# Split activations 192 instead of 64 bytes past the weight slots' phase, token-major weight tiles 192 bytes into their slots, one weight tile for both mLSTM gates

## What is computed

```python
def mlstm_mixer(h, w_in, w_if, b_if, head_norm, w_o):
    q, k, v, o_pre = jnp.split(h @ w_in, [hq, 2 * hq, 2 * hq + hv], axis=-1)
    gates = (h @ w_if + b_if).astype(jnp.float32)       # 1024 -> 2 * 4 heads
    gates = GATE_CAP * jnp.tanh(gates / GATE_CAP)
    log_i = _to_chunks(gates[..., :ML_HEADS], ML_HEADS, 1)[..., 0]
    log_f = _to_chunks(jax.nn.log_sigmoid(gates[..., ML_HEADS:]), ML_HEADS, 1)[..., 0]
    ...
def sqrelu_mlp(h, w1, w2):
    return jnp.square(jax.nn.relu(h @ w1)) @ w2
```

## Time and profile before

| | |
|---|---|
| median of 3 runs | 1549.48 us (1549.19 to 1552.05) |
| the profiled execution | 1549.48 us, its span 1547.7 us |
| PE busy | 1537.4 us (99%), 12836 matmuls |
| DVE, ACT, POOL busy | 1044.9 us (68%), 849.9 us (55%), 122.8 us (8%) |
| DMA | 281.05 MB, 182 GB/s on average |
| granted TensorE clock | 1.00 in every stretch of the windows shown |

### The profile page before, as it was taken

One profiled execution on the slowest core, in us unless ns is written; L12 is line 12 of the kernel. 1 busy time (PEld: TensorE's weight loads), 2 busy tenths in 40 slices (PEclk: granted clock), 3 DMA queues, 4 the chain that ended last, 5 costly groups with the idle time before them and its releaser, 6 DMA issues.

```text
span 1547.7 us, 35180 instructions
## 1 busy us (share of the span) xinstructions
PE 1537.4 (99%) x12836; PEld 1497.8 (97%) x12836; DVE 1044.9 (68%) x1765; ACT 849.9 (55%) x1301; POOL 122.8 (8%) x123
## 2 busy tenths in 40 slices
PE   9999999999999999999999999999999999999999
PEld 8899999988999999999999999999999988999999
DVE  7777765643876557666788766668566666687764
ACT  6776654546655445445445544556555547665543
POOL 1830000036000000000000000000000023200000
DMA  7146556554555566666665665656556981066664
GB/s 253 62 134 195 194 188 202 172 169 147 182 197 195 188 197 190 196 193 199 195 208 190 197 194 192 205 181 204 193 193 195 224 219 66 15 203 191 194 200 150
DMA packets 80784, 281.05 MB, mean 182 GB/s; under 512 B 8880, under 2 KB 12464, under 8 KB 80688
## 3 DMA queue, kind: packets, MB, share of 16 engines
q1 hardware_dynamic: 76800, 274.82, 55.3%
q10 hardware_dynamic: 3888, 4.85, 1.7%
HBM read 278.06 MB, written 1.57 MB: 181 GB/s over the span
## 4 chain that ended last, share of the span: by engine, by line
PE 95%; DVE 3%; ACT 1%; issue 1%; POOL 0%; ACTq 0%; DVEq 0%; POOLq 0%
PE psum L1760 27%; PE psum L1764 27%; PE psum L1761 27%; PE psum L1902 2%; PE psum L1904 2%; PE psum L1903 2%; PE psum L2194 1%; PE psum L2145 1%; PE psum L2259 1%; PE psum L2178 1%; PE psum L2090 0%; PE psum L1967 0%; PE psum L1957 0%; DVE w_lo L1039 0%; PE psum L1974 0%
## 5 line engine op out<-in xcount | busy, mean ns | idle before, releaser
L566 ACT ACTIVATE w_hi<-raw 128x1024 fp32r<-128x1024 f32 x518 | 547.2, 1058 | 478.8 <-PE psum L1764 421.7
L1039 DVE TENSOR_TENSOR w_lo<-raw,w_hi 128x1024 fp32r<-128x1024 f32 x483 | 590.5, 1223 | 246.2 <-ACT w_hi L566 245.8
L1760 PE MATMUL psum<-xs,w_hi 128*128 128x256 f32 x1912 | 530.7, 278 | 0.0
L1761 PE MATMUL psum<-xs,w_hi 128*128 128x256 f32 x1912 | 528.3, 276 | 0.0
L1764 PE MATMUL psum<-xs,w_lo 128*128 128x256 f32 x1912 | 528.2, 276 | 0.0
L1760 PEld LDWEIGHTS psum<-xs,w_hi 128*128 128x128 f32 x1912 | 358.9, 188 | 0.5 <-DVE w_lo L1039 0.2
L1761 PEld LDWEIGHTS psum<-xs,w_hi 128*128 128x128 f32 x1912 | 358.9, 188 | 0.3
L1764 PEld LDWEIGHTS psum<-xs,w_lo 128*128 128x128 f32 x1912 | 358.8, 188 | 0.0
L1764 PE MATMUL psum<-hs,w_lo 128*128 128x256 f32 x1280 | 353.3, 276 | 0.0
L1760 PE MATMUL psum<-hs,w_hi 128*128 128x256 f32 x1280 | 353.3, 276 | 0.0
L1761 PE MATMUL psum<-hs,w_hi 128*128 128x256 f32 x1280 | 353.3, 276 | 0.0
(11 more groups left out here) (292 smaller groups left out, 1487.4 us busy)
## 6 DMA issues: line engine op xcount, KB each, us to landing
raw<-tiles SPq DMA_DIRECT2D x518, 512.0 KB, 4.2
bias<-bias_dram ACTq DMA_DIRECT2D x8, 256.0 KB, 8.3
x<-x_in SPq DMA_DIRECT2D x4, 256.0 KB, 5.1
w1c_all<-w1c_k ACTq DMA_DIRECT2D x4, 256.0 KB, 4.4
w1c_all<-w1c_v ACTq DMA_DIRECT2D x4, 256.0 KB, 5.1
y_out<-x SPq DMA_DIRECT2D x8, 128.0 KB, 3.4
con<-consts SPq DMA_DIRECT2D x1, 803.0 KB, 8.8
bias_dram<-bias_row ACTq DMA_DIRECT2D x1, 512.0 KB, 7.1
```

Of the source, the lines that this page charges most:

```text
L566: act.activation(w_hi[s][:, :], raw[s][:, :], ACT.Copy).then_inc(hi_ready, 1)
L1039: dve.tensor_tensor(w_lo[s][:, :], raw[s][:, :], hi_of(w_hi[s][:, :]), ALU.subtract).then_inc(lo_ready, 1)
L1760: pe.matmul(out, w_hi[s][:, c:c + P], x_hi, start=first, stop=False)
L1761: pe.matmul(out, w_hi[s][:, c:c + P], x_lo, start=False, stop=False)
```

## The change

- Two spare regions of the layout change: `w_hi` and `w_lo` slots grow from 4096 to 4352 bytes (`SLOT`), `sil` is now the first two buffers of `half` (2048 bytes less), and `apart` shrinks by 128 bytes. The slots still begin at 128 modulo 256; `os_`, `xs`, `hs` and `arena` now begin at 64, which is 192 past the slots.
- Tiles of token-major stages lie 192 bytes into their slots (`TILE_AT`, `ASIDE`), so at phase 64, that of the activations. The first four tiles of kv and of nq stay at the slot's start. Of the 486 token-major matmuls 96 work on those.
- The offset from the activations to the moving operand changes so: in the feature form, moving minus stationary was 64 and is 192. In the token-major form it was 192 and is 0 (64 for the 96).
- Both gates come from one tile (`gates`: input gates in columns 0 to 3, forget gates in columns 32 to 35), so from one PSUM bank, at partitions 0 and 32. 517 tiles are left. mgate and mqk are one `feature` call of nine outputs, in which the gates' tile is paired with the first mqk tile.

```diff
+F_GATES = 32
-    ("mgate", 2, 2), ("mqk", 8, 8), ("mv", 8, 4), ("mo", 8, 4), ("wo_m", 8, 8),
+    ("mgate", 1, 1), ("mqk", 8, 8), ("mv", 8, 4), ("mo", 8, 4), ("wo_m", 8, 8),
...
+SLOT = TILE + 64
+ASIDE = 48
+TILE_AT = {}
 for _name, _tiles, _outs in STAGES:
     TILE0[_name], OUT0[_name] = N_TILES, N_OUTS
+    if _name in ("uk", "uq", "uv", "mv", "mo", "kv", "nq"):
+        for _t in range(RING if _name in ("kv", "nq") else 0, _tiles):
+            TILE_AT[N_TILES + _t] = ASIDE
+def slot_part(buffer, t):
+    first = TILE_AT.get(t, 0)
+    return buffer[:, first:first + TILE]
...
-        w_hi = [sb(f"w_hi{s}", [P, TILE], F32R) for s in range(RING)]
-        w_lo = [sb(f"w_lo{s}", [P, TILE], F32R) for s in range(RING)]
+        w_hi = [sb(f"w_hi{s}", [P, SLOT], F32R) for s in range(RING)]
+        w_lo = [sb(f"w_lo{s}", [P, SLOT], F32R) for s in range(RING)]
-        sil = [sb(f"sil{s}", [P, S]) for s in range(2)]
+        sil = half[0:2]
-        sb("apart", [P, 120])
+        sb("apart", [P, 88])
...
-                act.activation(w_hi[s][:, :], raw[s][:, :], ACT.Copy).then_inc(hi_ready, 1)
+                act.activation(slot_part(w_hi[s], t + RING * q if isinstance(q, int) else t), raw[s][:, :], ACT.Copy).then_inc(hi_ready, 1)
-                    dve.tensor_tensor(w_lo[s][:, :], raw[s][:, :], hi_of(w_hi[s][:, :]), ALU.subtract).then_inc(lo_ready, 1)
+                    dve.tensor_tensor(slot_part(w_lo[s], t_), raw[s][:, :], hi_of(slot_part(w_hi[s], t_)), ALU.subtract).then_inc(lo_ready, 1)
...
-                for o, (dst, b) in enumerate(((m_ti, "b_i"), (m_tf, "b_f"))):
-                    k = OUT0["mgate"] + o
-                    dve.wait_ge(tile_done, TILE0["mgate"] + o + 1)
-                    dve.tensor_tensor(dst, bank(k % 4, 0, S, slice(0, MH)), rb[0:MH, :], ALU.mult).then_inc(out_read, 1)
-                    dve.wait_ge(out_read, k + 1)
+                k = OUT0["mgate"]
+                dve.wait_ge(tile_done, TILE0["mgate"] + 1)
+                for dst, first in ((m_ti, 0), (m_tf, F_GATES)):
+                    rows = slice(first, first + MH)
+                    ins = dve.tensor_tensor(dst, bank(k % 4, 0, S, rows), rb[rows, :], ALU.mult)
+                ins.then_inc(out_read, 1)
+                dve.wait_ge(out_read, k + 1)
+                for dst, b in ((m_ti, "b_i"), (m_tf, "b_f")):
                     dve.tensor_scalar(dst, dst, vec[0:MH, VEC[b]:VEC[b] + 1], None, ALU.add).then_inc(m_gates, 1)
-                    take_lo(TILE0["mgate"] + o + RING)
+                take_lo(TILE0["mgate"] + RING)
...
-                    s, col = (t0 + n // 2) % RING, n % 2 * 512
+                    s, col = (t0 + n // 2) % RING, TILE_AT.get(t0 + n // 2, 0) + n % 2 * 512
...
-                feature("mgate", 2, "mix_1", norm_="mix_1", odd=True)
-                feature("mqk", 8, "mix_1")
+                feature("mgate", 9, "mix_1", norm_="mix_1", odd=True)
```

More of the change, by code:

```diff
@@ L482, in take_lo @@
                 if t in PACKED:
-                    (hi, lo), (exact, _) = packed_parts(w_hi[s], t), packed_parts(raw[s], t)
+                    (hi, lo), (exact, _) = packed_parts(slot_part(w_hi[s], t), t), packed_parts(raw[s], t)
                     pool.tensor_tensor(lo, exact, hi.bitcast(F32), ALU.subtract).then_inc(lo_ready, 1)
                 else:
-                    pool.tensor_tensor(w_lo[s][:, :], raw[s][:, :], w_hi[s][:, :].bitcast(F32), ALU.subtract).then_inc(lo_ready, 1)
+                    pool.tensor_tensor(slot_part(w_lo[s], t), raw[s][:, :], slot_part(w_hi[s], t).bitcast(F32), ALU.subtract).then_inc(lo_ready, 1)
             def stage(h, first):
@@ L755, in mlstm @@
                 root("mix_1")
-                used("mgate", 2)
+                used("mgate", 1)
                 used("mqk", 2)
@@ L1033, in take_lo @@
                     dve.wait_ge(lo_ready, t + RING * q)
+                t_ = t + RING * q if isinstance(q, int) else t
                 dve.wait_ge(hi_ready, q * RING + (t + 1))
-                if isinstance(q, int) and t + RING * q in PACKED:
-                    (hi, lo), (exact, _) = (packed_parts(b, t + RING * q) for b in (w_hi[s], raw[s]))
+                if t_ in PACKED and isinstance(q, int):
+                    (hi, lo), (exact, _) = packed_parts(slot_part(w_hi[s], t_), t_), packed_parts(raw[s], t_)
                     dve.tensor_tensor(lo, exact, hi_of(hi), ALU.subtract).then_inc(lo_ready, 1)
                 else:
-                    dve.tensor_tensor(w_lo[s][:, :], raw[s][:, :], hi_of(w_hi[s][:, :]), ALU.subtract).then_inc(lo_ready, 1)
+                    dve.tensor_tensor(slot_part(w_lo[s], t_), raw[s][:, :], hi_of(slot_part(w_hi[s], t_)), ALU.subtract).then_inc(lo_ready, 1)
             def clear_sums(name):
@@ L2337 @@
     mqk = 2 * MH * MQK
+    gates = np.zeros((D, F_GATES + MH), np.float32)
+    gates[:, :MH], gates[:, F_GATES:] = w_if[:, :MH], w_if[:, MH:]
     kv = a["w_kv_2"].reshape(D, 3, 2, G, DH)
@@ L2350 @@
         feature_tiles(mlp1[0]), feature_tiles(mlp2[0]),
-        narrow_tile(w_if[:, :MH]), narrow_tile(w_if[:, MH:]), feature_tiles(m_in[:, :mqk]),
+        narrow_tile(gates), feature_tiles(m_in[:, :mqk]),
         token_tiles(m_in[:, mqk:mqk + MH * MV]), token_tiles(m_in[:, mqk + MH * MV:]), feature_tiles(a["mlstm_w_o"][0]),
```

## The result

The changed kernel takes **1591.18 us** (median of 4 runs, 1590.02 to 1592.71), the kernel before beside it 1549.65 us. The ratio is 1.0268 (95% interval 1.0254 to 1.0282): 41.5 us slower, where 28 us less were forecast. It is rival D, whose sum was 1592 us.

A forecast was written before the change was run, and what follows sets the result against it. PE, busy for 1537.4 of 1547.7 us, was taken as the bound, so only its matmul steps count. 2.8 + 22.0 + 3.5 = 28.3 us off 1549.5 gave 1521.2 us; range 1481 to 1555 us.

The forecast's parts named there:

- rival D: Feature form at 192: reads meet as in mqk, long step in all layers, +45 us, 1592 us in all; chance 0.20.
- Part 1: At the gates: one tile less, 24 matmuls fewer at 117.7 ns, -2.8 us on PE's own path.
- Part 2: Feature form, offset 64 to 192: steps of 113.3 and 117.7 ns both fall to 111.7, -22 us.
- Part 3: Token-major form, offset 192 to 0: half the excess (9 ns) goes for 390 matmuls, nothing for 96, -3.5 us.
- Part 4: Copies, splits, `sil` in `half` and float32 work in `arena`: the last about 1 us either way, nothing taken.
- A: Both forms lose the full excess: feature step 108.4 ns, token-major 215, 68.6 us less, 1481 us; chance 0.13.
- B: Only a part gained, long steps vanish or token-major alone gains: 5 to 14 us, about 1540 us; chance 0.15.
- C: Phases do nothing, the two steps come from something else; only the gate tile counts, 1546.7 us; chance 0.14.
- the prediction's estimates of 109.2 and 215.8 ns: Skill's 262 and 518 cycles at 2.4 GHz for 256 and 512 columns, leaving 4.1 and 17.6 ns per matmul.

The follow-up runs named there:

- e2_gate: The kernel before with the one gate tile alone, slots, offsets and scratch unchanged: 1546.91 us, ratio 0.9983.
- the sweep: Separate burst kernel, PE alone: feature matmuls at eight operand offsets behind 0 to 3 small products, then token-major ones; feature steps 113.3 to 120.0 ns.
- k1: The changed kernel (offset 192) without any odd matmul, the small 60-column product at layer starts: 1563.14 us, ratio 1.0077.
- k2: The kernel before (offset 64) without any odd matmul: 1586.08 us, ratio 1.0233.
- o44_192: The changed kernel with odd matmuls of 44 columns instead of 60, beginning at PSUM column 468 instead of 448: 1551.77 us, ratio 1.0009.
- e1_back64: The changed kernel with its spacer back at 120 words, so feature offset 64 again, token-major offset still 0: 1546.12 us, ratio 0.9976.
- b3_64_mqk44: The kernel of e1_back64 with only the odd matmul ahead of mqk at 44 columns instead of 60: 1545.94 us, ratio 0.9978.
- b2_64_44: The kernel of e1_back64 with all odd matmuls at 44 columns instead of 60: 1546.22 us, ratio 0.9981.
- m3_widths: Separate burst kernel, PE alone: up_0's head, then a small product of 0 to 128 columns, offsets 64 and 192; at 192 short from width 4.
- run 201: Not a run label: "run" is a verb here, and 201 ns is the first of the steps listed for m3_widths at 192 with 60 columns.

## Why the prediction was wrong

**What bounds the kernel** was read rightly. PE sets the time, without gaps, and a change of the step goes straight into the total: 40.9 us by counted steps, 40.5 in the span.

**Part 1** (-2.8 us) was right: `e2_gate` measured -2.65. The chain of the gates wasn't late either: DVE was done at 324.07, and PE came to `turn_rows` (now L2038) at 327.39. DVE after, and PE:

```profile
308.75 0.83 DVE L1385 TENSOR_TENSOR arena<-psum,rb 4x256 f32<-4x256 f32 x2
309.62 0.60 DVE L1389 TENSOR_SCALAR arena<-arena,vec 4x256 f32<-4x256 f32 x2
...
323.67 0.40 DVE L1404 TENSOR_TENSOR arena<-arena 4x256 f32<-4x256 f32 x1
...
327.39 0.41 PE L2038 MATMUL psum<-con,arena 4*128 4x4 f32 x4
```

**Part 2** (-22 us) is the step that failed. It took 111.7 ns, the step of passes with little to stream, "the nearer load-bound row", for what the new offset would give. That row shows what a load needs, and nothing on which offset reaches it: the sweep has none below 113.3. The sweep's lowest steps, 113.3 ns for 256 columns and 226.7 for 512, each with one load, are as one to two. So the floor goes with the columns moved, which is an inference from these two shapes, and the load was not what bounded the short step. The kernel before stood at the floor already, and the earlier trace rows were not a slow and a half-slow place but the two states of one offset. The text itself said that its observation "doesn't say in which direction 192 goes" and still gave most of the chance to one direction. With a floor of 113.3 the most to be won from part 2 was 926 x 4.4 = 4 us, against 45 to be lost.

**Rival D** was right in its size and in one of its two reasons: the long step in all layers, 10,250 x 4.4 = 45 us against 43 measured for the offset alone. That the odd matmuls suit the old phase is what `k1`, `k2` and `o44_192` show. The same product holds the short step at 64 and the long one at 192. What spoke for D in the profile was that up_0 and mqk run in different steps at one and the same offset, with the same odd matmul behind different heads (mqk's has the one-column products of the earlier trace rows): the state depends on a layer's start, which the change leaves as it was while it moves everything around it. That deserved more than 0.20. D's other reason was not good, that at 192 the reads meet as in mqk, with the token-major rows as witness: in the feature form 192 reaches 113.3 ns too.

**Part 3** (-3.5 us): the direction was right, the term more than twice too large. The step fell to 226.7 ns for the 390, by 6.6 instead of 9, and to 228.9 for the 96, where nothing was taken: 390 x 6.6 + 96 x 4.4 = 3.0 us if every one of them followed another in the stream. Many stand behind a wait or another product. The float32 pass of 215 ns, taken as the bound below, was not one that this form reaches. Summed from start to next start over all 486, the form takes 117.7 us after and 119.2 before, so -1.5 us. Even that isn't all kept: `e1_back64` has 1.3 us less in it than `e2_gate` and 1.2 us more in the float32 products, and the two medians differ by 0.8 us with intervals that overlap.

**Part 4** (nothing): no sign against it. In the kernel after, where `arena` has moved to 64, the float32 products take 0.1 us more than before. The 1.2 us more in `e1_back64` can't be laid on the phase of `arena`, which is the old one there.

**Rivals A, B and C** fell with the sweep. By the Trainium skill ("TensorE: Matmul & The Clock Gate", section "Step-by-step: what each phase is for") a load of the next weights takes no read bandwidth from the running matmul; by that rule, as the prediction read it, phases mean nothing and C would have come. The runs don't agree with this reading: with PE alone at work the same instructions take 113.3 to 120.0 ns by their offset. No step of the sweep comes down to the prediction's estimates of 109.2 and 215.8 ns either.

The best kernel of the study has the one gate tile and leaves the activations at 64: `b3_64_mqk44`, `e1_back64` and `b2_64_44`, 1545.9 to 1546.2 us, 0.2% under the kernel before. `e2_gate`, at 1546.9, is hardly behind.

## What to carry to other kernels

Where the same instruction has two step times at different places of one kernel, ask first what switches between them, and count a change of layout as moving the switch too; the faster of the two may be the floor, and a burst kernel with only that instruction, swept over the offset, tells so in one run. It didn't tell which of the two steps a whole kernel takes; that has to be measured in the kernel itself. A layout and the small instructions placed around it are one setting and have to be tuned together. A floor taken from another shape of instruction is a bound for the range, not a value for the sum.

## What the runs showed of the hardware

- 256-column fp32r matmuls, each with a weight load, follow each other in 113.3 to 120.0 ns by the byte offset between the two operands modulo 256 (the weights at one phase), with no other engine at work and the clock at 1.00; 512-column ones in 226.7 (offset 0) to 234.2 ns. For the latter the bursts foretell the whole kernel: 226.7 and 228.9 ns at the kernel after's two token-major offsets in both, and 233.3 at the old one.
- At offsets 64 and 192 the same stream has two steady steps, 113.3 and 117.8 ns. PE keeps the one with which it begins over 1,528 matmuls, through tile changes and waits that are already met. It can change at a wait of some 0.7 us, and not always to the same one (`b2_64_44` and `b3_64_mqk44` at 12 us). At 192 a 44-column product instead of a 60-column one at the start of the layers, 20 PSUM columns further on, is worth 39 us of 1591.
- The state is sometimes not reached at once. In `m3_widths` at 192 with 60 columns the steps run 201, 120, 116, 116, 114, 114, 113, 113 ns before they stay at 113.3; at 64 they are at their value within the first four.
